# A two-block transformer kernel on one core: the triangular solve of the delta rule by 64x64 quarters, and the score and logit matmuls of two heads issued in pairs

## What is computed

```python
# gated delta rule, chunks of C = 64 tokens, 8 chunks, 4 heads
A = jnp.where(strict, jnp.einsum('bhnik,bhnjk->bhnij', kb, k) * decay, 0.0)
T = lax.linalg.triangular_solve(A + eye, jnp.broadcast_to(eye, A.shape), left_side=True,
                                lower=True, unit_diagonal=True)
u = jnp.einsum('bhnij,bhnjv->bhniv', T, v * beta[..., None])
w = jnp.einsum('bhnij,bhnjk->bhnik', T, kb * jnp.exp(g)[..., None])
...
# attention scores, and the index logits of the second block
s = jnp.einsum('brhnqd,brhnkd->brhnqk', qs, kb) * (D ** -0.5)
logits = jnp.einsum('bqhd,bsd->bqhs', iqb, ik32) * (IDX_DIM ** -0.5)
score = jnp.einsum('bqh,bqhs->bqs', iwb, jax.nn.relu(logits))
```

## Time and profile before

| | |
|---|---|
| median of three runs | 3181.61 us (3181.59 to 3187.2) |
| the profiled execution's own time | 3177.61 us |
| its span in the trace | 3175.6 us |
| granted TensorE clock, mean over the span | 0.962 |
| TensorE matmuls busy (share of the span) | 3011.6 us (95%) |
| VectorE, ScalarE, GpSimd busy | 39%, 36%, 39% |
| matmul records of the solve: L2059, and its transposes L2061 and L2063 | 1280, and 96 |
| score records (L1961) and logit records (L1864) | 256 and 128 |

### The profile page before, as it was taken

The page is one execution under the profiler, slowest core; times in us unless marked ns, Lnnn a source line. Parts: engine busy times, 40 slices in busy tenths (PEclk is TensorE's granted clock), DMA queues, the critical chain, the costliest instruction groups (busy, mean ns, idle before and its releaser), DMA issues.

```text
span 3175.6 us, 42194 instructions
## 1 busy us (share of the span) xinstructions
PE 3011.6 (95%) x14156; PEld 2368.0 (75%) x14156; DVE 1252.0 (39%) x2240; ACT 1147.7 (36%) x1894; POOL 1246.4 (39%) x626
## 2 busy tenths in 40 slices
PE   9998899999999989999999998999999999999997
PEld 7767877788877678778888656678878656688876
DVE  4455426553064444265521467330012557330012
ACT  4453134443234522344433223542233223542331
POOL 3313123555432131235554343145553343145553
PEclk9999899999999988999999989999999989999999
DMA  3211012223311100112333111122222111022222
GB/s 128 67 41 34 1 40 67 93 94 100 104 64 66 40 27 1 47 67 93 99 99 100 56 47 54 34 73 93 92 93 86 58 44 60 31 72 97 92 93 93
DMA packets 62869, 217.35 MB, mean 68 GB/s; under 512 B 6577, under 2 KB 6705, under 8 KB 62481
## 3 DMA queue, kind: packets, MB, share of 16 engines
q1 hardware_dynamic: 62416, 214.48, 20.4%
q0 software_dynamic: 320, 1.12, 0.1%
HBM read 213.48 MB, written 2.10 MB: 68 GB/s over the span
## 4 chain that ended last, share of the span: by engine, by line
PE 80%; DVE 7%; POOL 4%; ACT 4%; issue 3%; DVEq 1%; ACTq 0%; DMA 0%; POOLq 0%; SPq 0%
PE bank L1758 48%; PE bank L2059 5%; POOL wL L681 3%; PE bank L1961 3%; PE bank L1932 2%; PE bank L1807 2%; PE bank L1785 2%; PE bank L1983 2%; PE bank L1933 2%; PE bank L1934 2%; PE bank L1864 1%; PE bank L1972 1%; ACT wH L850 1%; PE bank L1815 1%; PE bank L1872 1%
## 5 line engine op out<-in xcount | busy, mean ns | idle before, releaser
L681 POOL TENSOR_TENSOR wL<-raw,wH 128x1024 fp32r<-128x1024 f32 x380 | 920.2, 2422 | 1409.0 <-ACT wH L850 1409.0
L1758 PE MATMUL bank<-hH,wH 128*128 128x512 f32 x1744 | 728.9, 418 | 23.4 <-POOL wL L681 17.6
L1758 PE MATMUL bank<-hL,wH 128*128 128x512 f32 x1744 | 687.2, 394 | 0.0
L1758 PE MATMUL bank<-hH,wL 128*128 128x512 f32 x1744 | 686.9, 394 | 0.0
L850 ACT ACTIVATE wH<-raw 128x1024 fp32r<-128x1024 f32 x380 | 399.4, 1051 | 278.6 <-PE bank L1758 238.3
L1758 PEld LDWEIGHTS bank<-hH,wH 128*128 128x128 f32 x1744 | 331.5, 190 | 164.1 <-issue 87.4
L1758 PEld LDWEIGHTS bank<-hL,wH 128*128 128x128 f32 x1744 | 331.5, 190 | 72.2
L1758 PEld LDWEIGHTS bank<-hH,wL 128*128 128x128 f32 x1744 | 332.4, 191 | 69.2 <-issue 10.5
L1758 PE MATMUL bank<-hidH,wH 128*128 128x512 f32 x864 | 338.1, 391 | 2.4 <-POOL wL L681 2.3
L1758 PE MATMUL bank<-hidH,wL 128*128 128x512 f32 x864 | 336.3, 389 | 0.0
L1758 PE MATMUL bank<-hidL,wH 128*128 128x512 f32 x864 | 336.3, 389 | 0.0
(11 more groups left out here) (323 smaller groups left out, 4287.1 us busy)
## 6 DMA issues: line engine op xcount, KB each, us to landing
raw<-w_dram SPq DMA_DIRECT2D x398, 512.0 KB, 3.4
x<-x_dram SPq DMA_DIRECT2D x4, 512.0 KB, 9.0
out_dram<-x SPq DMA_DIRECT2D x1, 2048.0 KB, 6.2
const<-const_dram SPq DMA_DIRECT2D x1, 1421.0 KB, 12.8
par_next<-par_dram POOLq DMA_DIRECT2D x5, 168.0 KB, 2.6
qkT<-pos_dram POOLq DMA_DIRECT2D x1, 256.0 KB, 7.0
const<-const_dram SPq DMA_DIRECT2D x1, 131.0 KB, 2.2
```

What stands on the lines that cost most here:

```text
L681: pool.tensor_tensor(wL[:, s, :], raw[:, s, :], wH[:, s, :].bitcast(F32), ALU.subtract).then_inc(w_lo.sem, 1)
L1758: mm = pe.matmul((out or ACC[bk])[:, :], wt[:, s, c:c + P], rhs, start=first and k == 0 and j == 0, stop=last and k == tiles - 1 and j == 2)
```

## The change

It has three parts.

1. **The solve by quarters.** In steps 1 to 18, 21 and 22 each matmul of a head becomes two, one for each chunk, on partitions 0 to 63 and on 64 to 127. In steps 1 and 4 to 18 both operands and the output of a chunk have 64 rows and 64 columns (rows 0 to 63 go to output partitions 0 to 63, rows 64 to 127 to 64 to 127); steps 2 and 3 keep the contraction over 128 and write 64 partitions each; step 21 has 128 moving columns, and step 22 has 128 weight columns, its second chunk in a bank of its own (`SIDE`). The zeros are no longer stored, so the matrices of four heads take 256 columns rather than 512, and VectorE, ScalarE and GpSimd work on 256. Step 0 still makes 128x128; its masking becomes two instructions of 64 partitions. Step 4 is a matmul by the identity rather than a transpose. Step 22's output is read by two instructions. The constants `causal` and `level` are halved, `unit` is added, and a filler tile grows by what they lose.
2. **Pairs.** Slot n of attention issues the scores of both heads when n is even, and none when it is odd; it waits until steps up to n-1 have been read. `index_logits` issues two heads at once, 16 pairs in place of 32 single ones, in four banks (PT, OA, STAT, TRO) rather than two; the table puts 2, 3, 3, 3, 3 and 2 pairs where 3, 6, 6, 6, 6 and 5 logits stood. `pool_mix` waits for the first 28 logits to be read, since its banks are among the four.
3. On TensorE the loop over the two layers of the first block is written out rather than a loop of the program.

The diff's core:

```diff
-for _u, _n in ((6, 3), (7, 6), (8, 6), (9, 6), (10, 6), (12, 5)):
+for _u, _n in ((6, 2), (7, 3), (8, 3), (9, 3), (10, 3), (12, 2)):
...
+        def index_bank(y):
+            pair = y // 2
+            return ((PT, OA), (STAT, TRO))[pair % 2 if pair < 14 else 0][y % 2]
+        SIDE = (bank[5], bank[6])
+        def by_chunk(ap):
+            return ap[:, 0:HN * CH].rearrange("p (h c) -> p h c", c=CH)
...
-                pool.tensor_tensor(eb[t % 2][:, :, :], ab[t % 2][:, :, :],
-                                   over_heads(cst("level", l * P, l * P + P)), ALU.mult).then_inc(lt_ready.sem, 1)
+                pool.tensor_tensor(eb[t % 2][:, :, 0:CH], ab[t % 2][:, :, 0:CH],
+                                   over_heads(cst("level", l * CH, l * CH + CH)), ALU.mult).then_inc(lt_ready.sem, 1)
...
-                                act.activation(mb[t % 2][:, :, :], heads(DB[e % 3][:, :]), ACT.Copy).then_inc(free.sem, 1)
+                                act.activation(mb[t % 2][:, :, 0:CH], by_chunk(DB[e % 3]), ACT.Copy).then_inc(free.sem, 1)
...
+                                for p0, src in ((0, DB[e % 3]), (CH, SIDE[t % 2])):
+                                    last = act.activation(dk[:, :, t * P + p0:t * P + p0 + CH], by_chunk(src), ACT.Copy)
...
-                E, A, X, XT = (r[t % 2][:, :, :] for r in (eb, ab, xb, xtb))
+                E, A, X, XT = (r[t % 2][:, :, 0:CH] for r in (eb, ab, xb, xtb))
...
-            def index_logits(w, y):
-                i, h = y // 8, y % 8
-                if y == 0:
+            def index_logits(w, pair):
+                if pair == 0:
                     pe.wait_ge(turn_done.sem, turn_done.at(w, 5))
-                if y >= 2:
-                    pe.wait_ge(ix_relu.sem, ix_relu.at(w, y - 1))
...
+                if pair >= 2:
+                    pe.wait_ge(ix_relu.sem, ix_relu.at(w, 2 * pair - 2 * (pair < 15)))
+                i = pair // 4
+                for y in (2 * pair, 2 * pair + 1):
...
                     pe.wait_ge(w_lo.sem, w_lo.at(w, WPOOL + 1))
+                    pe.wait_ge(ix_relu.sem, ix_relu.at(w, 28))
...
-                    pe.matmul(SC[n_ % 2][:, 0:P * (i + 1)], q[h * HD:h * HD + HD, f, i * P:i * P + P],
-                              k[h * HD:h * HD + HD, f, 0:P * (i + 1)], start=True, stop=True).then_inc(sc_done.sem, 1)
+                if n < 32 and n % 2 == 0:
+                    pe.wait_ge(sc_read.sem, sc_read.at(w, n))
+                    f, i, _ = att_step(n)
+                    for h in range(2):
+                        pe.matmul(SC[h][:, 0:P * (i + 1)], q[h * HD:h * HD + HD, f, i * P:i * P + P],
...
+                    for p0 in (0, CH):
+                        ch, cols = slice(p0, p0 + CH), slice(t * P + p0, t * P + p0 + CH)
+                        o = out[ch, h * CH:h * CH + CH]
+                        lt, x_, xt, m = (r[ch, h, 0:CH] for r in (LT, X, XT, M))
...
+                        elif k == 22:
+                            o, two = (SIDE[t % 2] if p0 else out)[:, h * CH:h * CH + CH], (A[ch, h, :], xt)
+                        mm = pe.matmul(o, *two, start=True, stop=True)
...
-            with pe.Fori(0, LAYERS) as L:
+            for L in range(LAYERS):
```

More of the change, by code:

```diff
@@ L181 @@
          ("cos1", S), ("sin1", S), ("count", S), ("turn1", P), ("turn2", P),
-         ("upto", P), ("even", 1), ("odd", 1), ("causal", P), ("level", 6 * P), ("icnt", 16)]
+         ("upto", P), ("even", 1), ("odd", 1), ("causal", CH), ("level", 6 * CH), ("unit", CH), ("icnt", 16)]
 CAT, _o = {}, 0
@@ L240, in constants @@
     put("odd", j // CH == 1)
-    put("causal", np.where(same & (j <= i), 0.0, NEG))
-    put("level", np.concatenate([(i // (2 * b) == j // (2 * b)) & (i // b % 2 == 1) & (j // b % 2 == 0)
+    r, t = np.arange(P)[:, None] % CH, np.arange(CH)[None]
+    put("causal", np.where(r <= t, 0.0, NEG))
+    put("level", np.concatenate([(t // (2 * b) == r // (2 * b)) & (t // b % 2 == 1) & (r // b % 2 == 0)
                                  for b in (1, 2, 4, 8, 16, 32)], axis=1))
+    put("unit", r == t)
     put("icnt", 1.0 / np.arange(1, 17, dtype=np.float32))
@@ L1161, in _ @@
                 for u in range(IN2):
-                    for y in IX_AT.get(u, ()):
+                    for y in (2 * pair + h for pair in IX_AT.get(u, ()) for h in range(2)):
                         wd = P * (y // 8 + 1)
@@ L1427, in delta_pre @@
                 e = ev_pre(t, k)
[L1428 to L1429 removed]
+                full, psum, free = heads(DB[e % 3][:, :]), by_chunk(DB[e % 3]), d_free[e % 3].sem
+                wide, wide_a = eb[t % 2][:, :, :], ab[t % 2][:, :, :]
+                E, A, X, XT = (r[t % 2][:, :, 0:CH] for r in (eb, ab, xb, xtb))
                 if k in (4, 5, 8, 11, 14, 17, 21, 22):
@@ L1690, in _ @@
                         gate_scale(w)
-                    for y in IX_AT.get(u + 1, ()):
+                    for y in (2 * pair + h for pair in IX_AT.get(u + 1, ()) for h in range(2)):
                         index_score(w, y)
@@ L2026, in delta_pre @@
                 e = ev_pre(t, k)
[L2027 removed]
+                side_free = [ev_pre(t - 2, 22)] if k == 22 and t >= 2 else []
+                out = start(w, e, *(ev_pre(t, o) for o in operands), *side_free)
                 tc = slice(t * P, t * P + P)
                 LT, A, X, XT, M = (r[t % 2] for r in (eb, ab, xb, xtb, mb))
[L2030 to L2035 removed]
+                if k == 2:
                     pe.wait_ge(l2_done.sem, l2_done.at(w, 8))
[L2037 to L2039 removed]
                 elif k == 4:
@@ L2056, in delta_pre @@
                 for h in range(HN):
-                    o = out[:, h * P:h * P + P]
-                    if h in two:
-                        mm = pe.matmul(o, two[h][0], two[h][1], start=True, stop=True)
-                    elif k == 4:
-                        mm = pe.transpose(o, XT[:, h, :], ident)
-                    else:
-                        mm = pe.transpose(o, (dk if k == 19 else dv)[:, h, tc], ident)
+                    wide = out[:, h * P:h * P + P]
+                    if k == 0:
+                        mm = pe.matmul(wide, gv[:, G_ + 4 * t + h:G_ + 4 * t + h + 1].broadcast_to([P, P]), cst("upto"),
+                                       start=True, stop=True)
+                        continue
```

92 lines of the change are left out of this document (48 added, 44 removed).

## The result

The changed kernel takes 3038.95 us (median of four runs, 3027.99 to 3052.44) against 3181.6 for the kernel before (3180.78 to 3187.2): ratio 0.955, 95% interval 0.951 to 0.959. The profiled execution took 3041.76. Its page, to be read against the earlier trace rows: TensorE's share and its part of the chain have not moved.

A forecast was written before the change was run, and what follows sets the result against it. TensorE was taken to bound the kernel, balanced in the first solve by one tile's chain. Solve 38, attention 32 and logits 16 made 86 off 3177.6 us, 3091.6, plus 4.0 for the median: 3095.6; range 3050 to 3152.

The forecast's parts named there:

- I take 0.040: Solve: a 64-column record on a quarter of the array costs 0.040 us, a two-tile step 1.28 us.
- Shorter evictions alone, or shorter matmuls alone, would give nothing; only both do: First solve: TensorE's records (1.78 us a step) and one tile's chain (1.78) balance, so both must shrink.
- first pair's term of 7.4: Solve, steps 5 to 18 of the first pair: 14 x (1.81 - 1.28) = 7.4 us less a layer.
- second's of 8.5: Solve, steps 5 to 18 of the second pair, between scans: 14 x (1.89 - 1.28) = 8.5 us less a layer.
- other five terms: Solve, a layer: steps 1 to 3 save 1.5, second pair's first steps 2.6, `level` 0.5; step 4 loses 0.8, steps 21-22 0.6.
- Four record lengths become three: Attention scores: the second head's first record runs beside the first head's second, saving 4.3 us in each of four stretches.
- The third step, 4 less for ScalarE: Attention: 36 us saved, less 4 for first-block slots where TensorE waits for ScalarE instead, leaving 32.
- 16 are left: Index logits, two layers: trips and streams save 22 us, VectorE takes 6 back, leaving 16.
- third rival: Solve: quarters run at the low clock or cost a full record, 0.11 us; slower, 3260 us; chance 0.08.
- No more TensorE idle time than before: Sign expected in the changed profile: TensorE idles no longer in the logits' stretch than before.
- Everything overlaps: First rival, all parts: quarter records at 0.027 us, paired heads at half; 126 us less, 3056 us; chance 0.18.
- second rival: Solve: quarters go one after the other, 0.054 us a record; total 3146 to 3157 us; chance 0.20.

The follow-up runs named there:

- e6_twice: The changed kernel with each quarter product of steps 5 to 18 issued twice: 3093.84 us, ratio 0.972 to the kernel before.
- e5_wide: The changed kernel with full-width evictions (512 columns) again in steps 4 to 18, quarter products kept: 3038.44 us, ratio 0.956 to the kernel before.
- e9_twin: The kernel before, loop written out, with 27 of 32 single logits each followed by the other head's product on the other 64 rows: 3159.74 us, ratio 0.993.
- e4_loop: The kernel before with only TensorE's loop over the layers of block 1 written out: 3172.82 us, ratio 0.999.
- e1: The kernel before with only the solve in quarters, half-width evictions and the written-out loop: 3125.70 us, ratio 0.985.
- e2: The kernel before with only the two heads' score matmuls issued together and the written-out loop: 3137.36 us, ratio 0.987.
- e10_again: The changed kernel run again unaltered, as a standard for later experiments: 3041.90 us, ratio 0.956 to the kernel before.
- e11_best: The changed kernel with projection scaling before index scores, the first mask and step 4's copies before the attention splits, and 46 warm-up products, not 30: 3012.67 us, ratio 0.946.

## Why the prediction was wrong, step by step

**Direction and mechanism were right. The overlap was sized too small in all three parts, the clock of the logits was put at nothing, and the range was too high with them.**

- *"I take 0.040"* for a record of a quarter failed, and with it the largest term of the sum, the solve's 38, which became 63. It is 0.029 (e6_twice). The two bounds that I took it from were those of quarters one after the other, 0.054, and of a full overlap, 0.027, and I went to the middle for want of a row. With 0.029 a step is 0.93 of records, and 1.02 was measured where 1.28 was forecast.
- *"Shorter evictions alone, or shorter matmuls alone, would give nothing; only both do"* failed. Shorter evictions alone do give nothing (e6_twice: 1.87 a step in the first solve, 1.81 before). Shorter matmuls alone give most of it (e5_wide: 1.27). My sum took the chain of one tile (0.89 + 0.20 + 0.69) as fixed, but most of it was records, so shorter records shorten it too. In the second solve no price of full-width evictions showed. The first pair's term of 7.4 became 11.0 (26.3 to 15.3), the second's of 8.5 became 10.9. The other five terms, 3.2 together, became 8 in that layer, with the scatter of 3; which of them failed was not taken apart. Of the 8, 5.3 are before step 5, where the granted clock went from 0.81 to 0.89.
- *"Four record lengths become three"* failed: they become two, since the second head's first record starts with the first head's first one. That is 8.6 a stretch of attention for 4.3, and attention gave 47 for 32. The 0.36 for a trip holds: 0.41 with logits of 384 columns, 0.39 with 512 (1755.62 to 1757.33 is 1.71, less 0.46 and 0.86). The third step, 4 less for ScalarE, was about right for the first block: of 2 x (16 x 0.36 + 8.6) = 28.8 there 24.4 came. In the second block, where nothing was taken off, 22.5 came; what holds back the other 6 was not looked for.
- *The index logits, "16 are left"*, failed most: 38. The overlap gives 8.6 a layer for 4.3. The rest is the clock. The prediction used, 0.50 for 8 us in this stretch, only as an argument for its third rival, and not as time that could come back. With a mean of 0.82 over 77 us, 14 us of the stage were lost to it, and 4 (0.94 over 59) afterwards. Trips and streams (14.4) and clock (10), less 3 us more of waiting, make 21 where 18.4 was measured. The clock's part is nearer 8: the twins, which change the clock and keep the trips, have stages of 69.0 on average, single logits of 76.8 (eight layers).
- *"No more TensorE idle time than before"* failed in the first layer: 9.6 us of waits in the stage, against 6.7. In the second they are 7.9 against 8.4. That VectorE would take some back, through the scaling behind two logits at once, was right: this wait grew from 2.7 to 8.6 and 6.9 us. The prediction did not count that the wait for ScalarE's reading of the logits (4.0 and 5.3) would go, so the 3 us a layer that it took off came in one layer only.
- *"The feed-forward parts must be the same to the microsecond"* failed, by 5.4 and 8.0 us. That of block 2's first layer stands at one of two lengths in 13 traces, 424 to 426 us (eight, granted clock 0.98 to 0.99) or 434 to 435 (five, 0.96). The five all have the solve in quarters, the eight are of both kinds; whether there is a link stays open.
- *The written-out loop* at 0 (e4_loop: 0.999) and the lengths of the evictions (0.44, measured 0.42 to 0.47; 0.38) were right. So was the solve's clock: 1.00 in the dense part of the first solve.
- *Two readings of rows* are off without moving the forecast: the loads in the earlier trace rows differ by 50 ns (low ends) and 51 (medians), not by 51 to 54, and at 0.083 a record the 28 steps lose 23 us, not 24.
- *The rivals.* "Everything overlaps" came true in every part, and its own sum, 126, was still too small by the clock of the logits (its 24 became 38) and by its solve (its 53 became 63); its attention (49) was right. The second rival did not come. The rule of the Trainium skill beside it, "TensorEngine Tiling (Array Packing)", Restrictions and Gotchas, that different row tiles cannot access the same PSUM bank at one time, is not what this case shows: the two quarters of a step write one bank, in different partitions, and run at 0.029 a record. By that rule the step would have been 1.73. The third rival, the low clock, was the wrong way round in the logits: the single ones had a granted clock of 0.71 to 0.91 (eight layers), pairs 0.91 to 0.97 (sixteen).
- *The range* ended at 3050, 6 us under the first rival's nominal time. That rival had 18 in 100, and its own terms could err by more than 6 us; the lower end should have been worked out from its bounds, not from its middle. The 0.2% that a measurement was said to tell is small too: the intervals here reach 0.2 to 0.4% to each side.

## What to carry to other kernels

Price a pair of matmuls on disjoint rows as one, and two quarters on the diagonal likewise, if they are neighbours in the stream; grouped by rows instead, they lost 23 us of the gain here, part of it by the clock. Where a stretch shows a low mean clock and works on part of the array, count that clock as time that may come back; one experiment (e9_twin) stands behind this. Before asking for shorter evictions, halve the records of the chain in thought: the chain may shrink with them.

## What was not expected of the hardware

**The start has two lengths.** The same instructions between the table loads at 9 and at 27 us take 18 us in nine traces and 28 to 30 in four (e1, e2, e6, e10). In both kinds TensorE idles for 0.9 to 2.6 us and then works (in e11_best it does not idle); in the one the granted clock stays at 1.00, in the other it is 0.50, the lower level of 1.2 GHz, for 27 to 31 us of dense work. What decides between them was not found; the length of the wait does not (1.0 to 2.6 us in the slow four, 0.9 to 2.6 in the others). The changed kernel's first trace and e10_again, the same program:

```profile
9.00:18.00 9.00, 6.46 (x44) 5.73 (x44) 3.00 (x4) 7.35 (x12) 2.34 (x1) 1.00 1.01 417
18.00:27.00 9.00, 8.87 (x60) 7.95 (x58) 0.00 (x0) 5.21 (x9) 2.08 (x1) 1.00 0.06 25
```

```profile
9.00:18.00 9.00, 6.95 (x30) 6.02 (x30) 3.01 (x4) 5.88 (x9) 2.35 (x1) 0.68 1.00 413
18.00:27.00 9.00, 9.00 (x32) 8.03 (x33) 0.00 (x0) 3.61 (x6) 0.00 (x0) 0.50 0.06 24
```

The 12 us of the start and the 8 to 10 of the feed-forward are together about as much as the 20 to 30 us by which runs of one kernel differ here; that they are its cause is argued, not shown. In the one trace with 46 warm-up products (e11_best) TensorE did not wait there and the clock stayed at 1.00, which nine traces in 13 do.

**The stage of single logits ran at a low clock, and with a twin of each on the other half of the array it did not** (0.71 to 0.91 against 0.98 and 1.00), though TensorE is busy for less of the time (85% of the stage against 94% in the two rows of e9_twin's section). A twin on the same 64 rows was not run, so whether it is the filled half or only the added product that does it stays open.
